# A 31-tap depthwise convolution on TensorE: 32 channels by 4 shifts becomes 16 channels by 8 shifts at every second position

## The reference, cut to what matters

```
u = glu(h @ pw1 + pw1_b)                  # 256 positions x 1024 channels
u = depthwise_conv(u, dw) + dw_b          # 31 taps per channel, causal: 30 zeros in front
u = layernorm(u, over the 1024 channels) * ln_w + ln_b
x = x + silu(u) @ pw2 + pw2_b
```

## Time and profile before

| what | us |
|---|---|
| median of 3 runs | 956.88 (956.66 to 957.69) |
| the profiled execution | 957.01 |
| its span in the trace | 955.2 |
| TensorE busy in the span | 922.0 |
| VectorE busy | 643.1 |
| ScalarE busy | 458.6 |

### The profile page before, as it was taken

The page is one execution under the profiler, slowest core; times in us unless marked ns, Lnnn a source line. Parts: engine busy times, 40 slices in busy tenths (PEclk is TensorE's granted clock), DMA queues, the critical chain, the costliest instruction groups (busy, mean ns, idle before and its releaser), DMA issues.

```text
span 955.2 us, 15426 instructions
## 1 busy us (share of the span) xinstructions
PE 922.0 (97%) x6358; PEld 793.3 (83%) x6358; DVE 643.1 (67%) x858; ACT 458.6 (48%) x658; POOL 73.6 (8%) x149
## 2 busy tenths in 40 slices
PE   6999999999999998999999999999999799999997
PEld 5888788899899988888788888888985688888886
DVE  5579788677768976746566656666755866665655
ACT  6445465434567444431454444445442655544453
POOL 6000000000110030000000000000553000000000
PEclk9999999999999999999999999999999899999999
DMA  9855444555665541000157655564893246566631
GB/s 325 250 183 176 132 161 149 176 176 181 227 199 175 178 133 45 2 1 3 48 174 228 204 185 177 180 205 150 252 232 83 78 165 220 176 196 204 198 108 45
DMA packets 106085, 152.42 MB, mean 160 GB/s; under 512 B 4114, under 2 KB 82464, under 8 KB 106016
## 3 DMA queue, kind: packets, MB, share of 16 engines
q1 hardware_dynamic: 101424, 141.19, 45.4%
q0 software_dynamic: 4272, 9.85, 3.8%
q10 hardware_dynamic: 320, 0.40, 0.1%
HBM read 145.58 MB, written 1.06 MB: 154 GB/s over the span
## 4 chain that ended last, share of the span: by engine, by line
PE 89%; DVE 5%; ACT 3%; issue 1%; DMA 0%; POOL 0%; SPq 0%; DVEq 0%; ACTq 0%; POOLq 0%
PE banks L1998 20%; PE banks L1948 14%; PE banks L1950 14%; PE banks L1949 14%; PE banks L1999 10%; PE banks L2351 4%; PE banks L2580 2%; DVE wl L1111 1%; PE banks L2433 1%; PE banks L2110 1%; ACT wh L658 1%; PE banks L2060 1%; PE banks L2134 1%; DVE x L1179 1%; PE banks L2444 1%
## 5 line engine op out<-in xcount | busy, mean ns | idle before, releaser
L1111 DVE TENSOR_TENSOR wl<-raw,wh 128x2048 fp32r<-128x2048 f32 x130 | 297.7, 2292 | 113.6 <-ACT wh L658 113.1
L1998 PE MATMUL banks<-x,wh 128*128 128x512 f32 x896 | 315.3, 394 | 1.2 <-DVE x L1179 1.1
L658 ACT ACTIVATE wh<-raw 128x2048 fp32r<-128x2048 f32 x132 | 252.1, 1912 | 133.3 <-PE banks L1950 90.8
L1999 PE MATMUL banks<-x,wl 128*128 128x256 f32 x896 | 250.6, 280 | 0.0
L1998 PEld LDWEIGHTS banks<-x,wh 128*128 128x128 f32 x896 | 168.2, 188 | 41.5 <-issue 4.7
L1999 PEld LDWEIGHTS banks<-x,wl 128*128 128x128 f32 x896 | 168.4, 188 | 1.2
L1948 PE MATMUL banks<-wh,yh 128*128 128x512 f32 x290 | 113.9, 393 | 1.1 <-DVE yl L1709 0.6
L1950 PE MATMUL banks<-wh,yl 128*128 128x512 f32 x290 | 112.5, 388 | 0.0
L1949 PE MATMUL banks<-wl,yh 128*128 128x512 f32 x290 | 112.5, 388 | 0.0
L1948 PE MATMUL banks<-x,wh 128*128 128x256 f32 x320 | 92.0, 288 | 1.8 <-DVE x L1179 1.7
L1949 PE MATMUL banks<-x,wh 128*128 128x256 f32 x320 | 90.0, 281 | 0.0
(11 more groups left out here) (381 smaller groups left out, 1251.4 us busy)
## 6 DMA issues: line engine op xcount, KB each, us to landing
raw<-in_l_ffn_up SPq DMA_DIRECT2D x32, 1024.0 KB, 5.5
raw<-in_l_ffn_down SPq DMA_DIRECT2D x32, 1024.0 KB, 5.0
raw<-in_w_in SPq DMA_DIRECT2D x29, 1024.0 KB, 5.2
raw<-in_l_w_in SPq DMA_DIRECT2D x13, 1024.0 KB, 5.1
raw<-in_l_pw SPq DMA_DIRECT2D x12, 1024.0 KB, 5.5
arena<-arena POOLq DMA_DIRECT2D x64, 71.0 KB, 4.5
raw<-in_w_out SPq DMA_DIRECT2D x4, 1024.0 KB, 5.1
raw<-in_l_w_out SPq DMA_DIRECT2D x4, 1024.0 KB, 5.0
```

Source lines behind the costliest of these rows:

```text
L658: nc.scalar.activation(wh[:, u % WBUFS, :], raw[:, u % RAWS, :], ACT.Copy).then_inc(E("hi_split"), 1)
L1111: nc.vector.tensor_tensor(wl[:, u % WBUFS, :], raw[:, u % RAWS, :], wh[:, u % WBUFS, :].bitcast(F32), ALU.subtract).then_inc(E("lo_split"), 1)
L1998: mm(outs[t], h[:, k, c], x2[:, k, :, :].rearrange("p w t -> p (w t)"), start=k == 0, stop=False)
L1999: ins = mm(outs[t][:, 0:T], l[:, k, c], xh[:, k, :], start=False, stop=k == KC - 1)
```

## The change

The 128 partitions now hold 16 channels at 8 shifts. A tap matrix (128x32) takes 8 taps of 16 channels, and its 32 columns are 16 channels for the even and 16 for the odd positions, so that a matmul moves 128 columns (every second position) and gives 256 outputs for each channel. Four such matmuls (`g`) add up the taps. There are again 256 matmuls of the convolution (512 records), 32 in a half, in four column groups, each with 128 moving columns in place of 256.

The rows: VectorE's `glu` writes even and odd positions apart, in two instructions a step. GpSimd stores a step's 256 rows to memory (`conv_rows`, one transfer), waits until it has landed, and reads them back in 8 transfers, one a shift, 16 partitions by 16 blocks by 140 positions (560 bytes) each.

The output of a matmul now has 32 partitions that mix 16 channels with two phases. VectorE puts that right with two rounds of 32x32 block transposes (`unmix`), one from the bank and one within on-chip memory. It then adds `ln_late` in a further instruction (`moved`). ScalarE's `taps_out` is gone: it adds the bias for two blocks in place, and makes `ln_late` for the six others.

Order: step 0's convolution moves behind pb3. `lnc` sums 256 channels rather than 512 and stands ahead of all of step 2. The column sums behind the last half are eight in place of four. The addition of `pw2b` to the residual (two instructions, line 1796) moves up into VectorE's step 2, and one of step 3's two tap builds moves ahead of `glu(3)`. The taps come from memory in one transfer, later, and are transposed by TensorE in 8 small instructions of their own (`vec2`) ahead of the unit `bkv`, in place of 8 transfers and two transposes at the start.

```diff
-SHIFTS = 4
-TAP_GROUPS = 8
+SHIFTS = 8
+TAP_GROUPS = 4
+PHASE = (T + PAD) // 2
+ROWS = T // 2 + SHIFTS // 2 * (TAP_GROUPS - 1)
...
             for i in range(4):
...
-                pool.wait_ge(E("glu"), i + 1)
+                pool.wait_ge(E("glu"), 2 * (i + 1))
+                pool.dma_start(conv_rows[2 * P * i:2 * P * (i + 1), :].rearrange("(j p) m -> p j m", p=P),
+                               upad[:, 2 * i:2 * i + 2, :, :].rearrange("p j e m -> p j (e m)")).then_inc(E("rows_stored"), 16)
+                pool.wait_ge(E("rows_stored"), 16 * (i + 1))
                 if i >= 3:
                     wait_full(pool, f"taps{i - 3}")
-                for q in range(4):
-                    for r in range(SHIFTS):
-                        pool.dma_start(shifted(i)[32 * r:32 * r + 32, :, q, 0:UCOLS - SHIFTS],
-                                       upad[32 * q:32 * q + 32, 2 * i:2 * i + 2, r:r + UCOLS - SHIFTS])\
-                            .then_inc(E(f"rows_shifted{i % 3}"), 16)
+                for r in range(SHIFTS):
+                    at = 2 * P * i * 2 * PHASE + r % 2 * PHASE + r // 2
+                    pool.dma_start(shifted(i)[16 * r:16 * r + 16, :, :],
+                                   bass.AP(tensor=conv_rows.tensor, offset=at,
+                                           ap=[[2 * PHASE, 16], [32 * PHASE, 16], [1, ROWS]]))\
+                        .then_inc(E(f"rows_shifted{i % 3}"), 16)
...
             def glu(i):
                 dve.wait_ge(E("glu_parts"), 4 * i + 4)
-                nc.vector.scalar_tensor_tensor(out=upad[:, 2 * i:2 * i + 2, PAD:PAD + T], in0=chunks(thb[:, 0, 0:512]),
-                                               scalar=1.0, in1=chunks(ytmp[:, 0, :]), op0=ALU.add, op1=ALU.mult)\
-                    .then_inc(E("glu"), 1)
+                for j in range(2):
+                    cols = slice(j * T, (j + 1) * T)
+                    nc.vector.scalar_tensor_tensor(out=upad[:, 2 * i + j, :, PAD // 2:].rearrange("p e m -> p m e"),
+                                                   in0=thb[:, 0, cols].rearrange("p (m e) -> p m e", e=2), scalar=1.0,
+                                                   in1=ytmp[:, 0, cols].rearrange("p (m e) -> p m e", e=2),
+                                                   op0=ALU.add, op1=ALU.mult).then_inc(E("glu"), 1)
...
                 scaled_out(chunks(thb[:, 0, 0:512]), f"pb{i}")
+                if i == 3:
+                    build_taps(3, 0)
                 glu(i)
                 if i < 3:
-                    build_taps(i)
+                    build_taps(i, 0)
+                build_taps(i, 1)
+                if i == 2:
+                    dve.wait_ge(E("pw2b_loaded"), 16)
+                    for s in range(NT):
+                        mark(nc.vector.tensor_tensor(xn[:, s, :], xn[:, s, :], pw2b, ALU.add))
...
+            def unmix(use, first, n):
+
+                mid = extra_t[:, first // 2 % 2, T * (first % 2):T * (first % 2) + n * T]
+                wait_full(dve, use)
+                for j in range(n):
+                    cols = slice(j * T, (j + 1) * T)
+                    ins = nc.vector.transpose(mid[:, cols].rearrange("p (n w c) -> p w n c", w=2, c=16),
+                                              bank(use)[:, cols].rearrange("p (w n c) -> p w n c", w=2, c=16))
...
+                wait_empty(dve, use)
+                sync()
+                nc.vector.transpose(acc[:, first:first + n, :].rearrange("p j t -> p (j t)")
+                                    .rearrange("p (n t e) -> p n e t", t=32, e=2),
+                                    mid.rearrange("p (n e t) -> p n e t", e=2, t=32)).then_inc(E("taps_unmixed"), 1)
...
+            def moved(first, n):
+
+                dve.wait_ge(E("ln_late"), first + n - 2)
+                nc.vector.tensor_tensor(acc[:, first:first + n, :], acc[:, first:first + n, :],
+                                        ln_late[:, first - 2:first - 2 + n, :], ALU.add).then_inc(E("ln_moved"), 1)
...
+            unmix("taps0", 0, 2)
+            dve.wait_ge(E("convolved"), 2)
+            nc.vector.tensor_tensor(ln_sums[:, 0:T], acc[:, 0, :], acc[:, 1, :], ALU.add).then_inc(E("ln_early_sum"), 1)
+            unmix("taps1", 2, 2)
...
+            nc.vector.tensor_tensor(pair(0), pair(0), on_pairs(ln_shift), ALU.subtract).then_inc(E("ln_centred"), 1)
+            moved(2, 2)
+            dve.wait_ge(E("ln_moved"), 1)
+            nc.vector.tensor_tensor(ln_sums[:, T:2 * T], acc[:, 2, :], acc[:, 3, :], ALU.add).then_inc(E("ln_late_sum"), 1)
+            dve.wait_ge(E("ln_squares"), 2)
             sq_sums = lnsq[:, 0:2, :]
+            mark(nc.vector.tensor_tensor(sq_sums, sq_sums, lnsq[:, 2:4, :], ALU.add))
             sync()
             nc.vector.tensor_tensor(ln_sq_sums, lnsq[:, 0, :], lnsq[:, 1, :], ALU.add).then_inc(E("ln_square_sum"), 1)
+            unmix("taps2", 4, 2)
+            moved(4, 2)
+            unmix("taps3", 6, 1)
+            moved(6, 1)
+            unmix("taps3b", 7, 1)
+            moved(7, 1)
...
             def conv_half(i, j, use, first, last):
+
+                if j == 0:
+                    pe.wait_ge(E(f"rows_shifted{i % 3}"), 16 * SHIFTS * (i // 3 + 1))
+                pe.wait_ge(E("taps_built"), 2 * i + j + 1)
                 out = take(use) if first else bank(use)
-                cols = slice(0, T) if first else slice(T, 2 * T)
-                for g in range(TAP_GROUPS):
-                    for q in range(4):
-                        ins = mm(out[32 * q:32 * q + 32, cols], tap_blocks(i)[:, g, 4 * j + q, :],
-                                 shifted(i)[:, j, q, SHIFTS * g:SHIFTS * g + T], start=g == 0, stop=g == TAP_GROUPS - 1)
+                taps = tap_blocks(i, j).rearrange("p (g b m) -> p g b m", g=TAP_GROUPS, m=32)
+                for w in range(2):
+                    at = (0 if first else T) + w * P
+                    for g in range(TAP_GROUPS):
+                        for q in range(4):
+                            ins = mm(out[32 * q:32 * q + 32, at:at + P], taps[:, g, 2 * q + w, :],
+                                     shifted(i)[:, 8 * j + 2 * q + w, SHIFTS // 2 * g:SHIFTS // 2 * g + P],
+                                     start=g == 0, stop=g == TAP_GROUPS - 1)
...
-                if i == 2:
-                    conv_taps(0)
+            conv_taps(0)
             conv_taps(1)
             ones = const("ones")
-            pe.wait_ge(E("taps_built"), 3)
-            pe.wait_ge(E("rows_shifted2"), 256)
-            conv_half(2, 0, "taps2", True, False)
             pe.wait_ge(E("ln_early_sum"), 1)
             give(mm(take("lnc")[:, 0:T], ones, ln_sums[:, 0:T], start=True, stop=True), "lnc")
-            conv_half(2, 1, "taps2", False, True)
+            conv_taps(2)
...
             conv_half(3, 1, "taps3b", True, True)
+            for n, first, count in ((2, 4, 2), (3, 6, 1), (4, 7, 1)):
+                pe.wait_ge(E("ln_moved"), n)
+                for c in range(first, first + count):
+                    ins = mm(sums, ones, acc[:, c, :], start=False, stop=c == 7)
...
+                pe.wait_ge(E("ln_squares"), n + 1)
+                for c in range(first, first + count):
+                    ins = mm(squares, ones, lnsq[:, c, :], start=False, stop=c == 7)
```

More of the change, by code:

```diff
@@ L79, in shape_constants @@
     put("upinc32", same32 & (i <= j))
-    put("eye32", (i % 32) == np.arange(32)[None, :])
+    put("eye16", (i % 16) == np.arange(16)[None, :])
     keep = at
@@ L182, in plan @@
         wide(f"bq{i}", "w_in", BQ + 256 * i, 2 + 2 * i)
+    s.use("vec2", 6)
     s.unit("T", "w_in", 0, BKV, s.use("bkv"))
@@ L991, in _ @@
             split_norm("n4", (2, 3))
-            def taps_out(i):
-                wait_full(act, f"taps{i}")
-                for j in range(2):
-                    c = 2 * i + j
-                    nc.scalar.activation(acc[:, c, :], bank(f"taps{i}")[:, j * T:(j + 1) * T], ACT.Identity, scale=0.5,
-                                         bias=vcol("l1_dw_b_2", c)).then_inc(empty(f"taps{i}") if j else E("convolved"), 1)
             for i in range(4):
                 next_unit()
-                if i == 3:
-                    taps_out(0)
                 for tag, dst, fn, scale, bias in (("pa", ytmp, ACT.Identity, 1.0, lambda c: vcol("l1_pw1_b_2", c)),
@@ L1011, in _ @@
                         nc.scalar.activation(h, h, fn, scale=scale, bias=bias(2 * i + j)).then_inc(E("glu_parts"), 1)
-            taps_out(1)
+            act.wait_ge(E("taps_unmixed"), 1)
+            for c in range(2):
+                nc.scalar.activation(acc[:, c, :], acc[:, c, :], ACT.Identity, bias=vcol("l1_dw_b_2", c))\
+                    .then_inc(E("convolved"), 1)
             wait_full(act, "lnc")
-            nc.scalar.activation(ln_shift, bank("lnc")[:, 0:T], ACT.Copy, scale=2.0 / DM).then_inc(empty("lnc"), 1)
-            mark(nc.scalar.activation(NMAX[:, 0:1], EPSL, ACT.Sqrt))
```

(46 more changed lines are left out.)

121 lines of the change are left out of this document (50 added, 71 removed).

## The result

The changed kernel takes 975.46 us (median of 4 runs, 974.10 to 977.44) against 956.77 for the kernel before in the same session: a ratio of 1.0204, 95% interval 1.0189 to 1.0219. It is 18.7 us slower, where 3 us faster was forecast, and lies far outside the range. The profiled execution took 975.45 us with a span of 973.6.

What follows compares the result with a forecast made beforehand. TensorE was taken to bound the stage up to the layernorm, a serial tail behind it. Last sum at 735.4 against 739.19 saves 3.8 us, 0.3 added for the clock: 957.0 - 3.8 + 0.3 = 953.5 us, range 950.5 to 958.6.

Steps and rivals of the forecast that it cites:

- Matmuls: Convolution on TensorE: records 27 ns apart in place of 53, so 13.8 us, 13.4 less.
- rival (3): Convolution on TensorE: a record keeps its 53 ns, 956.9 us, no change; chance 0.07.
- Transposes: VectorE's unmixing: priced like plain elementwise instructions, 0.42 us for 256 elements and 0.69 for 512.
- issues: GpSimd's eight reads of a step: 0.63 us an issue, bounds 0.53 and 0.92, 5.0 us together.
- the eight sums: Column sums on TensorE behind the last half: 3.4 us and 0.16 for the last's end, ending at 735.4.
- The products: VectorE's `glu`: two instructions of 256 elements, overlapped to 0.75 us against 0.69 before.
- rival (4): VectorE: strided instructions cost double, each `glu` 0.75 us more, kernel at 956 to 957.5 us; chance 0.10.
- Rows through memory: Step 3's store and eight reads: landing 3.5 us, issues 5.0, 3.0 behind the last issue, rows at 727.3.
- TensorE behind pb3: TensorE's end of stage: waits about 6 us before `lnc`, then for step 3's rows until 727.3; sums end at 735.4.
- rival (2): Slow row round trip: landings 4.8 us, issues 0.92, step 3's rows at 732.8, kernel at 959.0; chance 0.16.
- Taken as nothing: Kernel start: small tap transposes and ScalarE's later taps copy cost nothing, 0.6 us if the cover is gone.
- Rival (5): TensorE's clock falls to 1.2 GHz for the waits, up to 2.8 us more, 956.3 us; chance 0.10.

Runs made afterwards that it cites:

- experiment 2: Changed kernel with half as many read rows, twice as long (1,120 bytes), same neighbouring partitions, timing only: 972.33 us, ratio 1.0165.
- experiment 6: Changed kernel with each read bringing one of sixteen blocks (convolution wrong), plus 64 unused bytes a partition behind `dwt`: 952.92 us, ratio 0.9966.
- experiment 5: Changed kernel with 64 unused bytes a partition behind the wide `dwt`: 971.53 us, ratio 1.0157.
- Experiment 8: Changed kernel with reads spread over partitions, 64-byte pad, stores issued by ScalarE, step 3's two weight splits and `pw2b` additions behind `glu(3)`: 953.02 us, ratio 0.9960.
- experiment 4: Kernel before with 448 unused bytes a partition behind `dwt`: 961.55 us, ratio 1.0052.
- 11: Kernel before with 64 unused bytes a partition behind `dwt`: 959.28 us, ratio 1.0027.
- 12: Kernel before with 96 unused bytes a partition behind `dwt`: 961.14 us, ratio 1.0052.

## Why the prediction was wrong

**Matmuls: right.** 27 ns from start to start, and the rule of the Trainium skill (TensorE: Matmul & The Clock Gate, Part 3, "What overlaps and what doesn't"), that a load overlaps a running matmul only when its row group differs, does not hold for these column groups: rival (3) is dead. **Transposes, issues, the eight sums: right** (0.77 and 0.71; 0.56 against the 0.63 taken; 756.37 - 752.65 = 3.7 us against 3.6). **The products** cost 1.04 to 1.12 and not 0.75, half again as much and not double: rival (4) in small, 0.8 us by `glu(3)`.

**Rows through memory: the step that failed.** Its words were "2048 rows of 560 bytes at half of that = 4.9 us, hidden behind the issues; at the full price of a row 9.7 us". Measured: 71 ns a row, 9.1 us for a step, not hidden: the last data come 7.6 us behind the last issue, where 3.0 were taken. Halving the price with the length was nearly right (126 ns for 1,120 bytes, 71 for 560, experiment 2); what was wrong is the price that was halved. The 76 ns of the earlier trace rows belong to copies inside the on-chip memory that fill 32 neighbouring partitions each; reads that fill 16 pay 126 for a row of about that length, and 46 for a half one when the 16 are spread. As rates, for 1.15 MB in the time of all engines: 240 GB/s in the earlier trace rows, 126 in the changed kernel, 142 with long rows, 195 with the reads spread. The upper bound, 9.7 us, happens to lie near the measured 9.1, but for another reason. What of the rest comes from reading memory in place of the on-chip memory, no run shows. Second, "TensorE behind pb3" took step 2 as not waiting for rows. It asked about the round trip of step 3 alone, though I had four of them in one queue, one after the other, and though the full transfer engines of the earlier trace rows were said to speak for rival (2). The text did name, among what would make it fail, "the earlier steps' rows, each waiting for a round trip in full queues, stop TensorE ahead of step 3": this is what happened, and it had no term and no chance. Rival (2) had the right sign and the right place and was too small by 16 us, because it delayed one round trip, and its 4.8 us for a landing are to be compared with 7.9 to 12.5.

The last chain, term by term, forecast against measured:

| | forecast | after | later by |
|---|---|---|---|
| `glu(3)` done | 715.15 | 719.98 | 4.8 (4.0 from ahead of the stage, 0.8 products) |
| store of step 3 issued, behind that | 0.65 | 5.3 | 4.7 (GpSimd still at step 2) |
| landing | 3.5 | 8.7 | 5.2 |
| eight issues | 5.0 | 4.5 | -0.5 |
| last data | 3.0 | 7.6 | 4.6 |
| from rows to last sum | 8.1 | 10.3 | 2.2 (1.7 of it half rate) |
| last sum | 735.4 | 756.4 | 21.0 |

"From ahead of the stage" is the 4.0 us that are lost before the product of step 0. Behind the last sum the span goes on for 973.6 - 756.37 = 217.2 us against 955.2 - 739.19 = 216.0, which with the 0.3 forecast for the clock closes the 22 us.

**What each cause is worth, by runs.** The data of the reads: 971.53 - 952.92 = 18.6 us, of which 9.1 (or 12.3, with the stage relieved) go with the neighbouring partitions and about 3 with the length of the row; the parts overlap and need not add up. The place of the later tensors: 975.46 - 971.53 = 3.9. The two come one behind the other down to 952.92, 0.6 below the forecast, so together they must give its 22.0 us and these 0.6; what they don't settle is the forecast's own sum, where terms cancel as said at experiment 6. **"Taken as nothing"** at the kernel's start was right for the tap transposes (0.71 us) and blind to the widened `dwt`. The product of step 0 starts 2.4 us later than in the kernel before in the padded kernel of experiment 5 and 0.7 later in that of 6, though their work up to there is the same. A single profile is that rough, so the 4.0 us of arrival are 0.7 for the transposes, about 2 to 3 for the place, and the rest can't be told apart.

**The clock.** Rival (5) was there too, as a consequence. Stretches of 5 us of the kernel after (length, then TensorE's busy time; the clock is the third number from the end), to set against the earlier trace rows:

```profile
730.00:735.00 5.00, 2.15 (x42) 1.99 (x46) 1.12 (x2) 0.77 (x3) 1.03 (x2) 0.50 0.29 79
735.00:740.00 5.00, 3.16 (x93) 2.81 (x84) 1.69 (x4) 0.00 (x0) 3.44 (x7) 0.88 1.04 139
740.00:745.00 5.00, 0.00 (x0) 0.00 (x0) 0.49 (x1) 0.63 (x1) 0.00 (x0) 0.80 0.80 93
745.00:750.00 5.00, 3.97 (x65) 3.38 (x66) 0.27 (x1) 0.00 (x0) 0.00 (x0) 0.51 0.00 1
```

Behind the waits of 7.59 and 7.87 us the granted clock is 0.50 of full speed, 1.2 GHz, while the next half of a step runs; behind the one of 5.32 it averages 0.75 over 720 to 725 us. 1.5 to 1.7 us are lost each time. Experiment 8 shows the same slow start behind its one wait of 4.35 us: 64 records in 3.64 us, the next 64 in 2.77. The idle gaps of the Trainium skill's rule cited in the prediction (TensorE: Matmul & The Clock Gate, "HAM oscillation") are here the waits for rows, and the trace agrees that work behind them starts at half rate.

**Open.** Why a tensor's place changes the speed of matmuls that read and write other tensors, and by which rule; the line of the 128x512 matmuls shows 2.9 of the 4.8 us in experiment 4, but 2.1 of 2.5 in 11, and in 12 4.4, where the whole span is only 2.1 longer. Which engine or port limits reads into 16 neighbouring partitions, no run isolates, nor how they slow a store. How much of the 9.5 us of experiment 8 is the moved weight loads was not tried. Whether the kernel before gains by a deferral in another place was not tried.

## What to carry to other kernels

Take the price of a transfer from one with the same destination: here the same bytes cost 1.5 times as much when a read filled 16 neighbouring partitions as when it filled every eighth, and doubling the length of the rows gave back only a ninth. Spread the partitions inside each read. Where several round trips share a queue and each waits for its own landing, add up all of them from the first, and ask what stands in front of the last producer: moving two weight splits and two additions gave back 9.5 us that a queue of its own for the stores did not. Moving a split moves the weight load behind it too: look where that load lands among the other transfers. And when a change widens a tensor, run the kernel before with the same bytes unused, before any other part of the difference is explained.

## What was not expected of the hardware

- The same 2048 rows of 560 bytes take 71 ns each when a read fills 16 neighbouring partitions and 46 ns when it fills every eighth: 9 to 12 us of the kernel.
- 64 to 448 unused bytes a partition ahead of other tensors in SBUF make the kernel before 2.5 to 4.8 us slower (0.3 to 0.5%); with 448 the lag grows over most of its length.
- One 286 KB store lands in 3.5 us beside a weight load, with 86% of the engines' time taken, and in some 8 to 13 beside weights and reads into 16 partitions, whichever queue it is in.
- Two products of 256 elements that write their result in two interleaved halves cost 638 ns each by the mean of eight, where VectorE's plain instructions of that size cost 420; 32x32 block transposes of float32 cost about as much as plain ones (433 ns for 256 against 420, 713 for 512 against 690).
